# Hybrid decoder step on one core: copies issued behind the sample values, softmax divided after the product, router fed from unscaled rows in halves

## The reference

```python
h = rmsnorm(x); q, k, v, u = split(h @ w_in)
# mixer A: 8 heads x 64, three dilated windows (128,1), (512,4), (2048,16) with T5 bias,
#          branch outputs merged by their softmax denominators
# mixer B: causal pooling over 2/4/8/16 positions, linear map per group
x += concat(A, B) @ w_out
x += cross_attn(rmsnorm(x), mem_k, mem_v, w_xq, w_xo)     # 4 heads x 256, 256 memory tokens
h = rmsnorm(x) * g_ff
logits = h @ w_router + b_router                          # 32 experts
top_v, top_i = top_k(logits, 4); gates = softmax(top_v)
x += sum over the 4 experts of gate * (swiglu_clamped(h @ w_gate_up[e] + b) @ w_down[e] + b)
y = rmsnorm(x)
# also returned: the key/value windows of prompt and samples (2048 rows each), pool states, memory keys/values
```

## Time and profile before

| | |
|---|---|
| median of 3 runs | 1409.87 us (1401.8 to 1410.43) |
| the profiled execution | 1409.75 us |
| its span, first to last instruction | 1408.0 us |
| mean granted TensorE clock | 0.968 |
| PE busy | 1255.7 us, 89% |
| DVE / ACT / POOL busy | 481.2 / 230.3 / 67.7 us |
| DMA moved | 557.14 MB, mean 396 GB/s |
| DMA share of 16 engines, main queue | 96.0% |

### The profile page before, as it was taken

How to read it: one execution, slowest core, us unless ns; L and a number is a source line. 1 busy time by engine, 2 the same in 40 slices (tenths; PEclk the granted TensorE clock), 3 DMA queues, 4 the chain that set the end, 5 groups by cost and what they waited for, 6 DMA issues and landing times.

```text
span 1408.0 us, 16530 instructions
## 1 busy us (share of the span) xinstructions
PE 1255.7 (89%) x6407; PEld 528.5 (38%) x6407; DVE 481.2 (34%) x1037; ACT 230.3 (16%) x448; POOL 67.7 (5%) x69
## 2 busy tenths in 40 slices
PE   7989877989897999998999989999899998999986
PEld 5444323456644433333333333333333333333332
DVE  2387888332326412312232122321223212132124
ACT  1334443211311110110110100110011010011102
POOL 2010000005007000000000000000000000000000
PEclk9999988999997999999999999999999999999998
DMA  9999999998989699999999999999999999999993
GB/s 339 353 381 363 399 397 379 361 370 306 360 354 344 254 431 427 427 429 426 429 428 429 429 429 429 428 430 427 430 427 430 427 429 428 429 429 429 429 428 158
DMA packets 51740, 557.14 MB, mean 396 GB/s; under 512 B 7021, under 2 KB 9301, under 8 KB 15885
## 3 DMA queue, kind: packets, MB, share of 16 engines
q1 hardware_dynamic: 50629, 553.04, 96.0%
q0 software_dynamic: 1072, 3.57, 0.6%
HBM read 552.02 MB, written 71.72 MB: 443 GB/s over the span
## 4 chain that ended last, share of the span: by engine, by line
DMA 55%; PE 35%; DVE 5%; ACT 2%; issue 1%; SPq 1%; DVEq 0%; ACTq 0%; PEldq 0%
DMA wide<-in_w_gate_up 49%; PE bank L1954 12%; DMA wide<-in_cache_v_win 3%; PE bank L1642 3%; PE bank L1983 2%; PE bank L1684 2%; PE bank L1749 2%; PE bank L1512 2%; PE bank L1508 1%; PE bank L1662 1%; DMA slim<-in_w_xq 1%; DMA slim<-in_w_xv 1%; ACT wide L787 1%; PE bank L1737 1%; PE bank L1791 1%
## 5 line engine op out<-in xcount | busy, mean ns | idle before, releaser
L1954 PE MATMUL bank<-wide,att 128*64 128x512 f32 x2048 | 463.3, 596 | 58.5 <-DMA wide<-in_w_gate_up 58.3
L1954 PEld LDWEIGHTS bank<-wide,att 128*64 128x64 f32 x2048 | 139.3, 136 | 362.5 <-issue 228.8
L1983 PE MATMUL bank<-slim,att 128*64 128x512 f32 x1024 | 226.8, 595 | 0.0
L1422 DVE TENSOR_SCALAR att<-bank 128x512 f32<-128x512 f32 x32 | 22.1, 691 | 469.0 <-PE bank L1954 469.0
L1983 PEld LDWEIGHTS bank<-slim,att 128*64 128x64 f32 x1024 | 70.6, 137 | 152.2 <-issue 149.2
L1401 DVE TENSOR_TENSOR x<-x,bank 128x512 f32<-128x512 f32 x68 | 46.6, 685 | 233.1 <-PE bank L1936 226.4
L980 ACT ACTIVATE att<-att 128x512 f32<-128x512 f32 x32 | 20.2, 630 | 517.6 <-DVE att L1422 517.6
L1936 PE MATMUL bank<-tb,att 128*128 128x512 f32 (+1 forms) x192 | 84.7, 611 | 1.8 <-ACT tb L989 1.3
L989 ACT ACTIVATE tb<-bank 64x512 f32<-64x512 f32 x64 | 37.8, 591 | 234.1 <-PE bank L1983 233.7
L1662 PE MATMUL bank<-slim,ta 128*128 128x512 f32 x128 | 57.8, 601 | 0.5 <-DMA slim<-in_w_xv 0.3
L1176 DVE TENSOR_REDUCE small<-wide 128x24 f32<-128x1536 f32 x28 | 49.1, 1753 | 1.0
(11 more groups left out here) (290 smaller groups left out, 1153.1 us busy)
## 6 DMA issues: line engine op xcount, KB each, us to landing
wide<-in_w_gate_up SPq DMA_DIRECT2D x128, 2048.0 KB, 25.4
slim<-in_w_down SPq DMA_DIRECT2D x64, 2048.0 KB, 22.0
out_k_win_sample<-in_cache_k_win SPq DMA_DIRECT2D x16, 2044.0 KB, 25.3
out_v_win_sample<-in_cache_v_win SPq DMA_DIRECT2D x16, 2044.0 KB, 22.9
wide<-in_w_in SPq DMA_DIRECT2D x8, 1024.0 KB, 15.8
wide<-in_cache_v_win SPq DMA_DIRECT2D x8, 1024.0 KB, 7.5
wide<-in_cache_mem_k SPq DMA_DIRECT2D x8, 1024.0 KB, 24.4
wide<-in_cache_mem_v SPq DMA_DIRECT2D x8, 1024.0 KB, 14.7
```

The lines of the kernel that those rows point to most:

```text
L1954: ins = M(bk[half[h], :], rows[:, k, :], wide[:, k, c:c + 512], start=False, stop=k == KC - 1)
L1983: ins = M(bank_y[half[h], :], aT[:, f % 4, f // 4, :], slim[:, f, 512 * h:512 * h + 512], start=f == 0, stop=f == KC - 1)
```

## The change

It has four parts.

1. **Copies and loads.** In the sample loop the copies are issued after the value window of sample b. `COPIES` goes from `[5, 1, 3, 1, 2, 2, 2, 2, 2, 2, 3, 2, 1, 3]` with 1 left over to `[4, 1, 3, 1, 2, 2, 2, 2, 2, 2, 3, 2, 2, 2]` with 2 left over: one piece less at the start, one more behind `w_router`, one less behind the first gate_up, one more behind the first w_down. The identity and the second prompt tile are loaded by ACT.
2. **Sample softmax.** `values` uses the undivided exponents as soon as ACT has them. The sums over keys are made by PE: 16 matmuls with one column of ones per sample, into a column of `sx_bank`. DVE takes only a reciprocal (`part_of_sum`). ACT divides while it copies the product (`keep`). The mask moves into `turn_values`: 8 matmuls of 64 columns against a masked `own` of 32 columns. The two all-reduces per sample on GpSimd become one. `late_v` is waited for only before the window rows that need it; `row(b+1, 2)` is issued behind `values(b-1)`, `turn_values` behind `unit_values`.
3. **Router.** PE turns the unscaled `x`, and the router's logits are scaled and biased in one DVE operation (`largest`). ACT scales the rows for the experts (`scaled_rows`) and makes the bf16 casts of tile 1; GpSimd keeps the subtractions. Tile 1: upper 512 columns of `xo` first, its square sum in two halves, its transposes and its logits in two halves of the contraction (`turned_half`, `route_half`). `slots` and the one-hot of tiles 0 and 2 are spread among these steps.
4. **First expert.** It starts when the first half of the gathered tokens is read.

```diff
-            load(sp, "ident", ident[:, :], i["c_ident"])
-            for t in (0, 2, 1):
+            for t in (0, 2):
...
                 if b in ROUND_AT:
                     slim_round(ROUND_AT[b])
-                else:
-                    copy(COPIES.pop(0))
 
                 bb, use = place(("pv", b - 1))
                 sp.wait_ge(bank_full[bb], use + 1)
                 window(vwin, i["cache_v_win"], b, v_in)
+                if b not in ROUND_AT:
+                    copy(COPIES.pop(0))
...
-                pool.wait_ge(zpart, b + 1)
-                nc.gpsimd.partition_all_reduce(zz, zs, P, bass.bass_isa.ReduceOp.add).then_inc(zall, 1)
...
+            def keep(b):
+                if b:
+                    b_, use = place(("pvt", b - 1))
+                    act.wait_ge(bank_full[b_], use + 1)
+                act.wait_ge(rz_in, b + 1)
+                ps, s = product(act, "pv", b)
+                A(kept, ps[:, :], ACT.Copy, scale=rz[:, b:b + 1]).then_inc(s, 1)
...
+            read_out(act, "xo", 0, 0), read_out(act, "xo", 0, 1)
+            root(16, P, x[:, 0, :], hn[:, 0, :])
+            read_out(act, "xo", 2)
+            root(18, NS, x[0:NS, 2, :], hn[0:NS, 2, :])
+            act.wait_ge(scale_in, 1)
+            scaled_rows(0, P, slice(0, KC)).then_inc(rows_in, 1)
+            act.wait_ge(scale_in, 2)
+            scaled_rows(2, NS, slice(0, KC)).then_inc(rows_in, 1)
+            act.wait_ge(rows_in, 2)
+            for c in (1, 2):
+                ins = A(hn[NS * c:NS * c + NS, 2, :], hn[0:NS, 2, :], ACT.Copy)
+            ins.then_inc(tall, 1)
+            read_out(act, "xo", 1, 1)
+            A(hn[:, 1, 512:D], x[:, 1, 512:D], ACT.Square, accum_out=meansq[:, 17:18]).then_inc(early_sum, 1)
...
+            residual("xo", 0)
+            scale_of(0, P, 9)
+            residual("xo", 2)
             gained("tr3", tb, gff, (0,))
+            scale_of(2, NS, 10)
+            residual("xo", 1, (1,))
+            dve.wait_ge(early_sum, 1)
+            V.tensor_scalar(stat[:, 36:37], meansq[:, 17:18], 1.0 / D, EPS, ALU.mult, ALU.add).then_inc(early_root, 1)
+            dve.wait_ge(loaded["brow"], 16)
             largest(0)
             gained("tr3", tb, gff, (2,))
             largest(2)
+            gained_half(1)
+            residual("xo", 1, (0,))
+            dve.wait_ge(squares, 11)
...
             slots(0)
+            tile_onehot(0, 0)
+            largest(1)
             slots(2)
...
+            tile_onehot(0, 2)
+            slots(1)
+            tile_onehot(0, 1).then_inc(onehot_in, 2)
...
             def values(b):
-                pe.wait_ge(prob, b + 1)
+                pe.wait_ge(sexp, b + 1)
+                pe.wait_ge(rz_in, b)
                 pe.wait_ge(v_in, 64 * (b + 1))
-                pe.wait_ge(late_v, b + 1)
                 ps, s = take(pe, "pv", b)
...
+                for kind in range(4):
+                    for t in range(DEC_T):
+                        n = NS if kind == 3 else P
+                        M(sx_bank[32 * t:32 * t + 32, b:b + 1], flat[0:n, kind, :], ones[0:n, 0:1], start=kind == 0, stop=kind == 3,
+                          tile_position=(0, 32 * t))
+                for k, kind in enumerate((0, 1, 2, 3)):
+                    if kind == 2:
+                        pe.wait_ge(late_v, b + 1)
...
+            read_out(pe, "xo", 0, 0), read_out(pe, "xo", 0, 1)
+            turned_rows(0)
+            tile1 = {1: take(pe, "xo", 1, 1)}
+            half_times(1, range(KC))
             pe.wait_ge(loaded["wr"], 16)
             route(0)
+            read_out(pe, "xo", 2)
+            turned_rows(2)
+            tile1[0] = take(pe, "xo", 1, 0)
+            half_times(0, range(KC // 2))
+            route(2)
+            read_out(pe, "xo", 1, 1)
+            turned_half(1)
+            pe.wait_ge(loaded["before"], 16)
+            position(0)
+            half_times(0, range(KC // 2, KC))
...
+            route1 = take(pe, "route", 1)
+            route_half(1)
+            position(2)
+            read_out(pe, "xo", 1, 0)
+            turned_half(0)
+            route_half(0)
             position(1)
...
-            pe.wait_ge(hparts_in, 2)
+            pe.wait_ge(hparts_in, 1)
             pe.wait_ge(onehot_in, 2)
+            pe.wait_ge(bf_in, 5)
             gather(0, 0)
...
-                pe.wait_ge(xe_in, n + 2)
+                pe.wait_ge(xe_in, 1 if first and i == 0 else n + 2)
```

More of the change, by code:

```diff
@@ new lines, in _ @@
+            for h in range(2):
+                c = slice(512 * h, 512 * h + 512)
+                link(scaled_rows(1, P, slice(4 * h, 4 * h + 4)))
+                A(hparts[1][:, 0, c], hn[:, 1, c], ACT.Copy).then_inc(bf_in, 1)
+            for part in (1, 2):
+                for h in range(2):
+                    c = slice(512 * h, 512 * h + 512)
+                    act.wait_ge(left_in, 2 * (part - 1) + h + 1)
+                    A(hparts[1][:, part, c], rest[:, c], ACT.Copy).then_inc(bf_in, 1)
@@ L1223, in _ @@
             share(DEC_B - 1, DEC_B, P * (UNITS[DEC_B - 1][1] + 1))
[L1224 removed]
+            shift(DEC_B - 1), part_of_sum(DEC_B - 2)
             for u in range(2):
@@ L1491, in _ @@
             pe.wait_ge(rb_rep, 1)
+            ps, s = take(pe, "toep")
+            M(ps[0:HEADS, 0:TOEP], rb, cb[:, 0:TOEP], start=True, stop=True).then_inc(s, 1)
             for kind in range(6):
@@ L1497, in _ @@
                 M(sx_bank[0:NS, 304 + 8 * t:312 + 8 * t], cb[:, c:c + NS], rb, start=True, stop=True)
-            ps, s = take(pe, "toep")
-            M(ps[0:HEADS, 0:TOEP], rb, cb[:, 0:TOEP], start=True, stop=True).then_inc(s, 1)
             for t in range(3):
```

254 lines of the change are left out of this document (138 added, 116 removed).

## The result

The changed kernel takes 1430.55 us (median of 4 runs, 1428.62 to 1431.3), the kernel before in the same comparison 1408.09 us (4 runs). The ratio is 1.017, 95% interval 1.0141 to 1.02: slower by 22 us, where 11 us less were forecast. The profiled execution took 1431.3 us, its span is 1429.5 us.

What follows compares the result with a forecast made beforehand. DMA, through the start of expert 1's weight stream, was taken to bound the kernel. Gains of 5.5 (up to the query product), 5.5 (router) and 0.3 (first expert), 11.3 us, gave 1398.5 us; range 1389 to 1409.

Steps and rivals of the forecast that it cites:

- The bound, and the stream: The end is fixed by when expert 1's weights start to stream without a gap, at 467.00 us before the change.
- signs of being wrong: DVE waiting for loop key windows, PE over 95% busy there, DMA busy up to the reload, or unchanged router length.
- A: Everything up to the query product: w_xq lands earlier, 4.9 + 2.1 - 1.5 = 5.5 us, bounds 2 and 8.
- at worst they eat the whole piece: Bound on new DMA holes at the start and in SP's waits for values: at most the 4.9 us piece.
- the hole at 250 us: DMA idle 2.1 us from 250 to 255 us; copies issued behind pass 6's value window would fill it.
- That is even: In the sample loop, the key window lands 20 us after the value window's issue; DVE needs it after 20.7 us.
- The third rival: Key windows behind two copies come late in the sample loop, DVE waits, DMA runs dry: 1419 us; chance 0.10.
- a dry DMA would itself take the backlog away: Argument against late key windows in the sample loop: idle DMA would clear the queue that delays them; no size given.
- DMA remains its bound: A sample loop pass stays bound by DMA: 7.8 MB at 390 GB/s, 20 us.
- The piece less: One 2.1 MB copy fewer issued in front of w_xq, worth 4.9 us at 428 GB/s.
- Softmax divided late: Sample loop softmax: DVE loses some 1.7 us a pass, PE gains 1.7 us a sample; no gain counted.
- B: The router's new order completes the one-hot earlier: 8.2 us at full clock, 4.2 at half, 5.5 taken.

Runs made afterwards that it cites:

- e1: Changed kernel with the sample loop's copies issued ahead of the value window again, all else kept: ratio 0.9996 to the kernel before.
- e2: Kernel before with only the copy order changed, copies issued behind the value window in the sample loop: ratio 1.0148 to the kernel before.
- e6: Changed kernel with the key windows of samples 3 to 7 issued by GpSimd on its own queue: 1423 us, ratio 1.0126 to the kernel before.
- e12: Changed kernel with SP issuing value window, then next key window after a wait for scores, then copies: 1425 us, ratio 1.0137 to the kernel before.
- e10: e7 with the old numbers of copies, five in the first lot: ratio 0.9955 to the kernel before.
- e7: e1 plus three router moves: ACT's tile 1 square sum, PE's last xo products and DVE's last addition go earlier. Ratio 0.9956 to the kernel before.
- e13: e1 with the old numbers of copies, five in the first lot, without further router moves: 1403.07 us, ratio 0.9977 to the kernel before.
- e3: e1 with the old router and first expert, so new softmax, loads and lots of copies only: ratio 0.9985 to the kernel before.
- e5: Changed kernel with at most one copy behind each value window, four copies moved behind the loop: 1437 us, ratio 1.0201 to the kernel before.

## Why the prediction was wrong

**The bound, and the stream.** Right. The end moved with the first weights of expert 1, and 941.0 to 943.4 us follow it in each of the seventeen traces. This is what made the experiments legible. Of the prediction's signs of being wrong, two came: DVE waiting for key windows in the loop, and a router of nearly unchanged length.

**The step that failed** is in A: "SP waiting for values with the copies not yet issued, can open new holes. I can't see them in this trace. [...] I take 1.5 us". It was 22 us of idle DMA in the loop, with the place of the copies as its cause (e1, e2). The bound "at worst they eat the whole piece" had no row behind it, and of the 3 us from which the 1.5 were taken 2.1 are the hole at 250 us, which the sum counts by itself. It took the waits of the old order as a measure of the new, though in the old order the copies filled SP's wait and hid its length. That length was in the trace: SP waits 102.9 us for values, up to 21.5 us at a time, and a pass is 20.7 us from value window to value window, while the value window and the key window without copies are 3.7 MB or 9 us of transfer. Two copies issued behind the value window just cover a pass of 20 us; a pass that has one copy (sample 1) or none (sample 3, before it `w_xv`) is not covered, and these have the two large holes.

**"That is even".** The third rival named the key windows, with 0.10 and 1419 us, the nearest of all to the time. The mechanism was real and in part the cause, but the smaller part, 5 to 6 us (e6, e12). Its two numbers were not even. The pass of sample 4 shows it, on DVE's timeline after the change:

```profile
223.37 1.22 DVE L1186 TENSOR_TENSOR wide<-wide,bank 128x1024 f32<-128x1024 f32 x1 [7.69 <-DMA wide<-in_cache_k_win]
```

The value window had gone out at 198.95 us. DVE was ready for the keys 16.7 us after it (223.37 - 7.69) and not 20.7, and had them 24.4 us after it and not 20. That value window went out on a nearly empty queue (share 0.04 and 0.11 from 190 to 200 us), so it needed no backlog, and "a dry DMA would itself take the backlog away" did not help. `w_xv` the prediction never followed: it lists what stands behind the copies for the key windows alone, and `w_xv` is issued behind them as well.

**"DMA remains its bound", 20 us a pass from 7.8 MB.** Wrong as an argument. A mean of bytes over a mean rate bounds a pass only if there is always something queued. The value window did land sooner, as forecast (5.3 us for its large loads, before 7.6, e1 7.5), and this gained nothing.

**The piece less, 4.9 us.** It gained nothing that the runs show (e10 against e7, e13 against e1). Its hole opened at 75 to 90 us, which the sum allowed for only with the 1.5 us above.

**The hole at 250 us, 2.1 us.** Filled, in e1 as well (1.03), where the copies are not behind the values. The order was thus not needed to fill it.

**Softmax divided late.** Costs and gains at nothing: right within the measurement (e3, 0.9985). The sums on PE took 0.71 us for 32 instructions, after an estimate of 1.7. This is below even the 0.84 us that sixteen took in the earlier trace rows, with the granted clock at 0.50 around both. These have one column and not 32; that this is the reason wasn't tried.

**B, the router, 5.5 us.** Mis-sized: some 2 us by the means of the traces, and 0.6 us in the changed kernel itself. The laying out put the second products of `xo` at 434 and their addition at 437, which is 35.7 and 38.7 us after the start of `xo`; they came 38.6 and 42.3 us after it, since the transposes of tile 1 and `position(0)` stand ahead of them on PE and `route(2)` waited for the gain. `early_sum` came as named, and held `largest(0)` for 3.83 us. The last logits are 3.59 us at half clock (0.50 from 465 to 471 us), as the lower bound had it, and PE waited 3.04 us ahead of them. Some of DVE's small instructions were also stretched beside GpSimd (below). With e7's moves PE still waits there for the gain (2.22 us).

**The chances.** Slower by over 1% had 0.06, for a change that reorders every large load of the stage that the profile calls DMA-bound. No row priced the holes, and a cost without a row was given 1.5 us and a bound of 4.9.

## What to carry to other kernels

A bulk transfer in front of a waiting issue is not only an obstacle to the load behind it, it is what the DMA engines do during the wait. Before moving it behind the wait, compute for each pass how long the issuer waits and how many bytes are queued at that moment, pass by pass and not as a mean, and follow every load that changes its place relative to the bulk, not only the one that the loop needs next. Where the total of bytes is fixed, judge by idle DMA time in the stage; the length of the loop and the waits for one buffer can improve while the kernel gains nothing (e5).

## What the runs showed of the hardware

**SP's issue takes longer behind queued transfers.** Eight loads of `w_xv` took SP 3.69 us in the trace of before, with two windows issued in the 7 us ahead of them. After the change, with two copies of 2.1 MB among these, they took 15.99 us, and in e5 the eight of `w_xq`, with eight copies and four loads of 1 MB issued in the 42 us ahead, 27.69 us. Whatever SP has to issue next waits too. At what depth this begins wasn't tried.

**Some small DVE instructions stretch beside GpSimd.** Timelines of the changed kernel, DVE and then GpSimd:

```profile
451.70 0.83 DVE L1332 CAST att<-idx 128x8 f32<-128x8 uint32 x1
...
455.24 1.84 DVE L1332 CAST att<-idx 32x8 f32<-32x8 uint32 x1
...
471.50 0.17 DVE L1332 CAST att<-idx 128x8 f32<-128x8 uint32 x1
```

```profile
450.37 2.13 POOL L720 TENSOR_TENSOR scr<-scr,mkT 128x1024 f32<-128x1024 f32 x1
...
454.93 2.12 POOL L727 TENSOR_TENSOR hn<-hn,mv 32x1024 f32<-32x1024 f32 x1
```

The same instruction takes up to 1.84 us beside GpSimd, and both stretched ones end when GpSimd's ends: 452.53 and 452.50, 457.08 and 457.05. It takes 0.17 us at 471.50, where one GpSimd instruction ends (471.58) and the next begins. In the trace of before it is the same: 1.18, 0.97 and 0.60 us, each ending within 0.03 us of GpSimd's. Not every instruction is hit: `MAX8` and `FIND_INDEX8` at 451.17 and 451.48, beside the same GpSimd instruction, take 0.20 and 0.18 us, as they do at 470.97 and 471.27 (0.20, 0.19). This agrees with the Trainium skill (SBUF — State Buffer, SBUF: two separate sides), which has VectorE, for some kinds of instruction, and GpSimd share a pair of ports that one of them holds for a whole instruction. In the router, where DVE's small instructions are the path, four such stretches add 4.6 us, not all of it on the path: 0.7 and 1.7 for these two, and 1.4 and 0.8 for two instructions on 128x1 elements at 462.25 and 463.92 (1.56 and 0.98 us, others of that size 0.15).

**A queue of its own is served beside a full one.** Key windows issued by GpSimd in e6 landed in 7.5 us, while copies and `w_xv` (26.2 us) stood in SP's queue. On SP's queue behind two copies they took 18.9 us, and ahead of the copies (e12) 8.7 us. The Trainium skill (DMA: Bandwidth & Descriptors, Queues, rings and completion order) says that each DMA engine goes round the queues that have work, packet by packet, and these landings agree with it.
